# Rotary steps of three attention heads moved from VectorE to GpSimd, and the query scale moved into a PSUM eviction

## The reference

```python
def axial_rope(x, rows, cols):            # latent tokens only
    ...
        x1, x2 = jnp.split(xh, 2, axis=-1)
        return xh * cos + jnp.concatenate([-x2, x1], axis=-1) * sin
...
def diff_attention(q, k, v, lam):
    scale = ATT_DH ** -0.5
        s = jnp.einsum('bqhad,bkhad->bhaqk', qblk, k).astype(F32) * scale
        p = jax.nn.softmax(s, axis=-1)
        a = p[:, :, 0] - lam * p[:, :, 1]
        return jnp.einsum('bhqk,bkhv->bqhv', a.astype(v.dtype), v)
...
            q = axial_rope(q, rows, cols)
            k = axial_rope(k, rows, cols)
```

## Time and profile before

| | |
|---|---|
| Time, median of 3 runs (lowest, highest) | 2919.29 us (2917.91, 2921.66) |
| Profiled execution: its own time, its span | 2919.1 us, 2917.0 us |
| Busy share of PE, DVE, ACT, POOL | 95%, 45%, 28%, 26% |
| Granted PE clock, mean of the span | 0.981 |

### The profile page before, as it was taken

How to read it: one execution, slowest core, us unless ns; L and a number is a source line. 1 busy time by engine, 2 the same in 40 slices (tenths; PEclk the granted TensorE clock), 3 DMA queues, 4 the chain that set the end, 5 groups by cost and what they waited for, 6 DMA issues and landing times. The chain is left out here.

```text
span 2917.0 us, 40368 instructions
## 1 busy us (share of the span) xinstructions
PE 2763.1 (95%) x16562; PEld 2640.3 (91%) x16562; DVE 1312.0 (45%) x2132; ACT 815.2 (28%) x1273; POOL 763.3 (26%) x336
## 2 busy tenths in 40 slices
PE   6997887999999999999899997899999999999997
PEld 5997677999999999999899996569999999999996
DVE  6698986743222222222557513545432222222225
ACT  5113665251111111111542232542511111111113
POOL 1572123531111111111322222334311111111113
PEclk9998999999999999999999998999999999999998
DMA  6443101411111111110325434324111111111101
GB/s 245 162 152 101 23 16 66 173 58 44 43 43 43 43 43 43 43 43 18 110 99 201 149 116 165 127 80 150 58 44 43 43 43 43 43 43 43 43 0 65
DMA packets 57724, 227.13 MB, mean 78 GB/s; under 512 B 7376, under 2 KB 17296, under 8 KB 47120
## 3 DMA queue, kind: packets, MB, share of 16 engines
q1 hardware_dynamic: 56032, 225.12, 21.8%
q10 hardware_dynamic: 1584, 0.51, 0.1%
HBM read 191.52 MB, written 29.88 MB: 76 GB/s over the span
## 5 line engine op out<-in xcount | busy, mean ns | idle before, releaser
L219 PE MATMUL ps<-hh,wi_hi 128*128 128x384 f32 x2112 | 707.2, 335 | 0.0
L221 PE MATMUL ps<-hh,wi_lo 128*128 128x384 f32 x2112 | 705.5, 334 | 0.0
L220 PE MATMUL ps<-hl,wi_hi 128*128 128x384 f32 x2112 | 705.4, 334 | 0.0
L1328 DVE TENSOR_TENSOR hid<-ps,hid 128x384 f32<-128x384 f32 x132 | 73.6, 558 | 987.2 <-ACT hid L1034 987.2
L219 PEld LDWEIGHTS ps<-hh,wi_hi 128*128 128x128 f32 x2112 | 396.4, 188 | 0.8
L220 PEld LDWEIGHTS ps<-hl,wi_hi 128*128 128x128 f32 x2112 | 396.4, 188 | 0.8
L221 PEld LDWEIGHTS ps<-hh,wi_lo 128*128 128x128 f32 x2112 | 396.4, 188 | 0.0
L1034 ACT ACTIVATE hid<-ps 128x384 f32<-128x384 f32 x132 | 64.9, 492 | 1126.3 <-PE ps L221 1126.3
L1162 POOL TENSOR_TENSOR wi_lo<-raw_in,wi_hi 128x2048 fp32r<-128x2048 f32 x44 | 203.0, 4614 | 648.4 <-ACT wi_hi L1024 648.3
L1339 DVE SCALAR_TENSOR_TENSOR x<-ps,mod,x 128x128 f32<-128x128 f32 (+1 forms) x704 | 327.1, 512 | 78.4 <-PE ps L221 74.2
L219 PE MATMUL ps<-hid_hi,wo_hi 128*128 128x384 f32 x1056 | 354.6, 336 | 2.8 <-DVE x L1339 2.7
(11 more groups left out here) (294 smaller groups left out, 4581.3 us busy)
## 6 DMA issues: line engine op xcount, KB each, us to landing
raw_in<-in_w_ffn_in_dram SPq DMA_DIRECT2D x44, 1024.0 KB, 4.8
wmt<-in_w_mod_t_dram SPq DMA_DIRECT2D x56, 512.0 KB, 3.5
raw_out<-in_w_ffn_out_dram SPq DMA_DIRECT2D x22, 1024.0 KB, 4.8
gla_spill<-turn SPq DMA_DIRECT2D x24, 576.0 KB, 2.9
oraw<-in_w_in_odd_dram SPq DMA_DIRECT2D x24, 512.0 KB, 4.7
wmt_odd<-in_w_mod_t_dram SPq DMA_DIRECT2D x24, 512.0 KB, 4.6
x<-in_x_dram SPq DMA_DIRECT2D x8, 1152.0 KB, 9.2
wm<-in_w_mod_dram SPq DMA_DIRECT2D x16, 512.0 KB, 11.0
```

What stands on the lines that cost most here:

```text
L219: pe.matmul(acc, w_hi, in_hi, start=first, stop=False)
L220: pe.matmul(acc, w_hi, in_lo, start=False, stop=False)
L221: return pe.matmul(acc, w_lo, in_hi, start=False, stop=last)
L1328: dve.tensor_tensor(hid[:, t], ps[:, 2 * t + 1, 0:CW], hid[:, t], ALU.mult).then_inc(hid_done, 1)
```

## The change

In `attention` the rotary steps of heads 1 to 3 leave DVE's list. POOL makes them instead, all six of a head in a row, ahead of everything else that POOL's list has for that head. In both functions the query scale of 1/8 leaves DVE: ACT applies it when it copies the query tiles out of PSUM. The rotary steps of head 0 in `opening` stay on DVE, as plain two-operand instructions.

```diff
@@ block.vector (attention)
-                def rope_times(h, n):
-                    src = (q_of, k_of)[n](h)
-                    dve.wait_ge((rot_q_in, rot_k_in)[n], 128 * h)
-                    if n == 0:
-                        dve.tensor_scalar(src[:, 0:CTX], src[:, 0:CTX], DH ** -0.5, None, ALU.mult)
-                    dve.scalar_tensor_tensor(out=src[:, lat], in0=src[:, lat], scalar=(DH ** -0.5, 1.0)[n], in1=cos[:],
-                                             op0=ALU.mult, op1=ALU.mult).then_inc(rope_part, 1)
...
-                        dve.wait_ge(signed, 1)
-                    if u in steps and h + 1 < HEADS:
-                        step, which = steps[u]
-                        step(h + 1, which)
@@ block.gpsimd (attention)
+                def rope(h, n):
+                    src, t = (q_of, k_of)[n](h), (turned_q, turned_k)[n]
+                    pool.wait_ge((rot_q_in, rot_k_in)[n], 128 * h)
+                    pool.tensor_tensor(src[:, lat], src[:, lat], cos[:], ALU.mult).then_inc(rope_part, 1)
+                    pool.tensor_tensor(t[:], t[:], sin[:], ALU.mult).then_inc(rope_part, 1)
+                    pool.wait_ge(rope_part, 4 * (h - 1) + 2 * n + 2)
+                    pool.tensor_tensor(src[:, lat], src[:, lat], t[:], ALU.add).then_inc(roped, 1)
...
+                pool.wait_ge(signed, 1)
                 for h in range(HEADS):
+                    if h + 1 < HEADS:
+                        rope(h + 1, 0)
+                        rope(h + 1, 1)
                     if h >= 1:
                         scales(h - 1)
                         normalise(h - 1)
@@ block.scalar (opening)
-                        act.activation(result[:, m, cs[c]], ps[:, NC * (m % 2) + c, 0:CW], ACT.Copy).then_inc(taken, 1)
+                        act.activation(result[:, m, cs[c]], ps[:, NC * (m % 2) + c, 0:CW], ACT.Copy,
+                                       scale=DH ** -0.5 if Q0 <= m < Q0 + HEADS else 1.0).then_inc(taken, 1)
@@ rope (opening)
-                        dve.tensor_scalar(src[:, 0:CTX], src[:, 0:CTX], scale, None, ALU.mult)
...
-                    dve.scalar_tensor_tensor(out=src[:, lat], in0=src[:, lat], scalar=scale, in1=cos[:],
-                                             op0=ALU.mult, op1=ALU.mult).then_inc(rope_part, 1)
+                    dve.tensor_tensor(src[:, lat], src[:, lat], cos[:], ALU.mult).then_inc(rope_part, 1)
```

More of the change, by code:

```diff
@@ L1534, in _ @@
             def _(dve):
-                def rope_times(h, n):
-                    src = (q_of, k_of)[n](h)
-                    dve.wait_ge((rot_q_in, rot_k_in)[n], 128 * h)
-                    if n == 0:
-                        dve.tensor_scalar(src[:, 0:CTX], src[:, 0:CTX], DH ** -0.5, None, ALU.mult)
-                    dve.scalar_tensor_tensor(out=src[:, lat], in0=src[:, lat], scalar=(DH ** -0.5, 1.0)[n], in1=cos[:],
-                                             op0=ALU.mult, op1=ALU.mult).then_inc(rope_part, 1)
-                def rope_turned(h, n):
-                    t = (turned_q, turned_k)[n]
-                    dve.scalar_tensor_tensor(out=t[:], in0=t[:], scalar=(DH ** -0.5, 1.0)[n], in1=sin[:],
-                                             op0=ALU.mult, op1=ALU.mult).then_inc(rope_part, 1)
[L1548 to L1551, removed]
                 def combine(n):
@@ L1603, in _ @@
                 dve.tensor_tensor(k_lo[0][:, 0:T], k_of(0), k_hi[0][:, 0:T].bitcast(F32), ALU.subtract).then_inc(qk_low, 1)
-                steps = {1: (rope_times, 0), 2: (rope_turned, 0), 3: (rope_sum, 0),
-                         4: (rope_times, 1), 5: (rope_turned, 1), 6: (rope_sum, 1)}
                 for n in range(UNITS + 2):
@@ L2158, in rope @@
                 def rope(n):
-                    src, turned, scale = result[:, (Q0, K0)[n]], turned_qk[n], (DH ** -0.5, 1.0)[n]
+                    src, turned = result[:, (Q0, K0)[n]], turned_qk[n]
                     if n == 0:
@@ L2164, in rope @@
                     if n == 0:
-                        dve.tensor_scalar(src[:, 0:CTX], src[:, 0:CTX], scale, None, ALU.mult)
                         dve.wait_ge(signed, 1)
-                    dve.scalar_tensor_tensor(out=src[:, lat], in0=src[:, lat], scalar=scale, in1=cos[:],
-                                             op0=ALU.mult, op1=ALU.mult).then_inc(rope_part, 1)
-                    dve.scalar_tensor_tensor(out=turned[:], in0=turned[:], scalar=scale, in1=sin[:],
-                                             op0=ALU.mult, op1=ALU.mult).then_inc(rope_part, 1)
+                    dve.tensor_tensor(src[:, lat], src[:, lat], cos[:], ALU.mult).then_inc(rope_part, 1)
+                    dve.tensor_tensor(turned[:], turned[:], sin[:], ALU.mult).then_inc(rope_part, 1)
                     dve.wait_ge(rope_part, 2 * n + 2)
```

## The result

The changed kernel took 2931.29 us (median of 7 runs, 2927.1 to 2934.89), the kernel before 2921.66 us on the same chip: a ratio of 1.0035, 95% interval [1.0025, 1.0044], some 10 us slower. (One of the 7 runs of the kernel before was disturbed, 3472.14 us; the ratio leaves it out.) The forecast was 2928.0 us, with 0.62 on slower.

What follows compares the result with a forecast made beforehand. DVE, the busiest engine in the attention units, was taken as the bound there, with a 6.0 us unit floor. From 2919.1 us, -6.1 + 1.9 + 4.0 + 5.3 + 3.8 = +8.9 gave 2928 us, range 2915 to 2936.

Steps and rivals of the forecast that it cites:

- Bound and place: Projection bound by PE, attention units busiest on DVE; the change acts in attention alone, the opening counting as nothing.
- Two turns: `combine` needs the shared port for `w`, then `prob`; a queued POOL step goes between: +1.9, +4.0 and +5.3 us.
- the two cases left open for head 1: Where `k_low` ends in head 1: POOL's step first costs 5.0 us, `prob` first 3.0; +4.0 taken.
- The removal: DVE loses 18 rotary steps and three small scalings in attention; units shrink to their floor, -6.1 us, bounds -4 and -7.
- 6.0 us is the floor of a unit: Attention units without a rotary step go round through PE and ACT in 6.0 us, so a unit shrinks no further.
- The prediction's own sign of being wrong: Units 1 to 6 staying above 6.3 us with DVE idle in them would mean the removal gave nothing.
- The clock: Stalls in attention bring PE half-clock stretches behind long units; two such stretches, +3.8 us, bounds 0 and 9.5.
- given by one stall in one: One stall in head 3 was followed by a half-clock unit 1.9 us over the floor, the price per stretch.
- Rival 1: In `combine`, DVE passes `w` and `prob` together, POOL not between; meetings cost 1.5 us, 2914.5 to 2915; chance 0.18.
- Rival 2: POOL keeps the port over cosine and sine steps, 4.7 us; some +4 in heads 1 and 2 each, 2936; chance 0.12.
- Rival 3: POOL's steps meet DVE only in idle time in attention; -6.1 us, 2911 to 2913; chance 0.08.

Runs made afterwards that it cites:

- e1: Kernel before with only the query scale moved to ACT's copies, rotary steps staying on DVE; 2921.82 us, ratio 1.0001 to the kernel before.
- e4: Changed kernel with the one-column product `w` made from one tensor operand and two one-column scalars; 2922.27 us, ratio 1.0004 to the kernel before.
- e3: Changed kernel with each POOL rotary step replaced by two fills that read nothing from SBUF; 2919.68 us, ratio 0.9991 to the kernel before.
- e5: Changed kernel with POOL's rotary steps spread over units, each released when its unit's scores are ready; 2919.43 us, ratio 0.999 to the kernel before.
- e6: e5 with `w` made from one tensor operand and two scalars, as in e4; 2918.65 us, ratio 0.9989 to the kernel before.

## Why the prediction was right, and which terms were not

**Bound and place.** Right. The projection did not move, the scaling gave nothing (e1), and the attention took 9.0 us more where 8.9 were forecast.

**Two turns.** Right in place, and in size as a sum. Forecast were `prob` or `w` of 3 to 4 us in units 1, 2, 7 and 8 of head 0, 0 and 8 of head 1, 0 and 1 of head 2. In seven of the eight `prob` was held: 3.47 to 3.50 us in the five wide units, 2.54 and 2.43 in the two short ones, which take 0.35 alone; unit 1 of head 2 kept 1.42. Against the lengths before, by the table:

| | forecast | measured |
|---|---|---|
| head 0, units 1, 2 | +1.9 | 0.77 + 1.02 = +1.8 |
| head 0, units 7, 8, head 1, unit 0 | +4.0 | 2.08 + 2.39 + 0.13 = +4.6 |
| head 1, unit 8, head 2, units 0, 1 | +5.3 | 4.22 + 1.03 - 0.21 = +5.0 |
| sum | +11.2 | +11.4 |

Of the two cases left open for head 1, POOL was first. At head 2 POOL was first twice in one `combine`: 4.2, 1.0 and -0.2 us where 2.2, 0.7 and 2.4 were forecast, so this line agrees in its sum alone, and that is luck. e4 shows the mechanism itself: with the need of a second turn taken away, 8.2 us come back.

**The removal.** The step that failed is "6.0 us is the floor of a unit", applied to all of units 1 to 6: -6.1 forecast, -2.3 measured in e3 (-3.7 without what half clock took back in head 0), outside the bounds of -4 and -7. The 6.0 came from units without side work. Units with 512 columns of it go round through DVE's side eviction and PE's transposes in 6.45 us, and before the change all but units 1 and 4 stood at their floors: in head 1, unit 2 at 6.47, unit 5 at 6.44, units 3 and 6 at 6.01 and 6.06. The prediction's own sign of being wrong, units above 6.3 with DVE idle in them, came in units 4 and 5. What shrank in e3 was unit 4 of each head (0.9 each) and unit 1 of heads 1 and 2 (0.5 each), 3.7 us; 1.4 of it went again in head 0's half-clock stretch. In the changed kernel itself unit 1 is held by POOL, and unit 4 alone shows.

**The clock.** The term of +3.8 was mis-sized too. Its sign came: there was more half clock, and stretches at 0.50 right behind long units (in the second half of unit 8 of head 0, and all through unit 0 of head 2). A mean grant of 0.95 over 223.1 us is some 22 us at 0.50 (twice 0.05 of it), 0.92 over 232.1 some 37. PE was busy 7.8 us longer for the same 1476 matmuls; but it idles 42 of 232 us here, and how much of the 7.8 went into idle time no run separates. In the units' lengths the 9.0 us are +11.4 in the eight units above, -2.7 in unit 4 of heads 0 to 2, -1.5 in head 3 (there `w` waited 0.97 us for `p_lo` instead of 2.54, which no term had) and +1.8 in all others, most of it in units 1 to 3, where the grant was below 1. So outside the stalls the clock brought at most some 1.8 us; with e3's removal instead, 9.0 + 2.3 - 11.4 leaves about 0. The price of 1.9 us "given by one stall in one" had no ground: the kernel before has such a stretch in unit 2 of head 2 as well, 7.99 us long, with no `w` or `prob` held ahead of it:

```profile
382.97:390.96 7.99, 4.76 (x31) 3.98 (x30) 6.40 (x10) 3.77 (x6) 4.50 (x6) 0.79 0.01 3
```

These two errors, of the removal and of the clock, are some 2 to 4 us each and have opposite signs: **the total is as near as it is because they cancelled**; the sum of the stalls alone was sized right.

**The rivals.** Rival 1 (`w` and `prob` pass together) fell with the `prob` of 3.5 us. Rival 2 (POOL keeps its turn over two steps) fell too: `prob` ran between the cosine and the sine step (310.01, 312.25), and no `prob` was longer than 3.50 us. Rival 3 is the e5 kernel, where the steps do lie in idle time: 0.999, not the 0.998 that its -6.1 would have made.

## What to carry to other kernels

Work moved from DVE to an idle POOL was not free here, because the two met at a shared port: count not the idle time of the new engine but the dependent instructions of the old one that need the port, since between two of them the other's queue got in once. With the same 18 instructions the kernel was 0.35% slower when they stood at the head of POOL's list, and 0.1% faster than before (interval 0.9981 to 0.9999, barely clear of 1) when they were released with DVE's reduces, which read PSUM. Before crediting a removal, find for each kind of iteration what ends it: a floor read from the iterations without side work is not the floor of the others.

## What was not expected of the hardware

- A one-column product with one tensor operand and two one-column scalars took 0.27 or 0.28 us in all 36 units of e4, also while POOL ran a `k_lo`; with two tensor operands it was held up to 2.41 us in the changed kernel and 2.56 in e5.
- POOL fills of 1024 columns (0.95 us each) held DVE's `prob` in no unit.
- Who goes first within 0.1 us can't be read from start times: `w` shows 376.98 and waited for a step that shows 377.01; in e4 a `prob` at 314.33 waited for a step at 314.36, but the one at 308.34 went ahead of one at 308.48. What decides was not tried.
- PE's half-clock stretches wander from unit to unit between kernels that differ elsewhere (unit 2 of head 1 took 6.47 us before, 8.03 in e3, 7.64 in e5 and 6.48 in e6, with no meeting in any of them), so that a single unit's length says little without its granted clock.
